# Reordering the decay blocks of a state-space scan on ScalarE and VectorE

## What is computed

```python
def ssd_scan(xs, dt, a, bm, cm, init_state):
    ...
    da_cs = jnp.cumsum(da, axis=-1)
    decay_in = jnp.exp(segsum(da))
    scores = jnp.einsum('bclhn,bcshn->bhcls', cc, bc) * decay_in
    y_diag = jnp.einsum('bhcls,bcshp->bclhp', scores, x)
    ...
    y = (y_diag + y_off).reshape(b, l, h, p)

def gated_rmsnorm(y, z, w):
    g = y.astype(jnp.float32) * jax.nn.silu(z.astype(jnp.float32))
    g = g.reshape(shape[:-1] + (SSD_GROUPS, SSD_WIDTH // SSD_GROUPS))
    g = g * lax.rsqrt(jnp.mean(g * g, axis=-1, keepdims=True) + EPS)
    return g.reshape(shape) * w.astype(jnp.float32)
```

## Time and profile before

| | |
|---|---|
| median of 3 runs | 763.07 us (762.62 to 763.31) |
| profiled execution | 761.61 us, span 759.9 us |
| TensorE busy | 723.8 us, 95% of the span |
| VectorE busy | 328.2 us, 43% |
| ScalarE busy | 215.9 us, 28% |
| GpSimd busy | 140.3 us, 18% |
| read from and written to HBM | 199.92 MB and 12.88 MB, 280 GB/s over the span |

### The profile page before, as it was taken

The page is one execution under the profiler, slowest core; times in us unless marked ns, Lnnn a source line. Parts: engine busy times, 40 slices in busy tenths (PEclk is TensorE's granted clock), DMA queues, the critical chain, the costliest instruction groups (busy, mean ns, idle before and its releaser), DMA issues.

```text
span 759.9 us, 10417 instructions
## 1 busy us (share of the span) xinstructions
PE 723.8 (95%) x3950; PEld 355.4 (47%) x3950; DVE 328.2 (43%) x880; ACT 215.9 (28%) x491; POOL 140.3 (18%) x234
## 2 busy tenths in 40 slices
PE   5999999999999999999999999999899899999995
PEld 4357553446445534433344755345544653443332
DVE  2022625647635552312471253474763555231157
ACT  2210155845024101011322024574602410111132
POOL 4146042220110100101102503322011011010112
PEclk9999999999999999999999999999999999999998
DMA  8999335997309799999896233497430379999962
GB/s 316 357 324 353 112 117 212 387 377 271 111 1 343 306 412 415 424 418 424 315 387 239 88 110 118 173 388 306 158 113 3 133 305 411 419 421 419 424 252 83
DMA packets 65655, 207.95 MB, mean 274 GB/s; under 512 B 8089, under 2 KB 8961, under 8 KB 53315
## 3 DMA queue, kind: packets, MB, share of 16 engines
q1 hardware_dynamic: 54936, 179.86, 61.2%
q10 hardware_dynamic: 5547, 16.12, 5.5%
q0 software_dynamic: 5120, 11.28, 4.4%
HBM read 199.92 MB, written 12.88 MB: 280 GB/s over the span
## 4 chain that ended last, share of the span: by engine, by line
PE 76%; DVE 9%; DMA 8%; ACT 3%; issue 2%; SPq 1%; POOL 1%; POOLq 0%; DVEq 0%; ACTq 0%
PE bank L2405 15%; PE bank L2290 11%; PE bank L2032 8%; PE bank L2420 7%; DMA arena<-in_w_up_dram 6%; PE bank L1976 6%; PE bank L2089 5%; PE bank L1897 4%; PE bank L2018 3%; DMA ring<-in_w_ada_dram 2%; PE bank L2134 2%; PE bank L2122 2%; PE bank L2396 2%; PE bank L2381 1%; PE bank L2106 1%
## 5 line engine op out<-in xcount | busy, mean ns | idle before, releaser
L2405 PE MATMUL bank<-ring,work 128*32 128x512 f32 (+1 forms) x640 | 114.2, 595 | 2.1 <-DMA arena<-in_w_up_dram 2.1
L2405 PEld LDWEIGHTS bank<-ring,work 128*32 128x32 f32 (+1 forms) x640 | 33.3, 120 | 73.8 <-issue 71.9
L1731 DVE COPY xs_tok<-bank 128x256 f32<-128x256 f32 x20 | 8.5, 425 | 135.5 <-PE bank L2412 135.5
L2420 PE MATMUL bank<-ring,xs_tok 128*64 128x512 f32 (+2 forms) x320 | 65.7, 597 | 1.0 <-DVE xs_tok L1731 1.0
L2032 PE MATMUL bank<-arena,ring 128*128 128x384 f32 x192 | 62.2, 486 | 0.0
L2405 PE MATMUL bank<-arena,work 128*64 128x512 f32 (+1 forms) x128 | 56.9, 597 | 0.0
L848 POOL DMA_INDIRECT gather_at<-h_rows,idx x18 | 18.2, 1013 | 173.1 <-PE bank L2396 130.7
L1897 PE MATMUL bank<-ring,cpad 128*32 128x512 f32 x384 | 49.7, 603 | 0.2 <-DMA ring<-in_w_ada_dram 0.2
L2032 PEld LDWEIGHTS bank<-arena,ring 128*128 128x128 f32 x192 | 36.5, 190 | 25.0
L1976 PE MATMUL bank<-ring,arena 128*128 128x512 f32 x96 | 42.8, 597 | 0.9 <-DVE arena L1278 0.5
L2290 PE MATMUL bank<-ring,arena 128*128 128x512 f32 x96 | 43.6, 597 | 0.0
(11 more groups left out here) (384 smaller groups left out, 1100.4 us busy)
## 6 DMA issues: line engine op xcount, KB each, us to landing
ring<-in_w_ada_dram SPq DMA_DIRECT2D x48, 1024.0 KB, 9.2
ring<-in_w_down_dram SPq DMA_DIRECT2D x28, 1024.0 KB, 14.1
ring<-in_w_gate_dram SPq DMA_DIRECT2D x24, 1024.0 KB, 12.1
ring<-in_w_up_dram SPq DMA_DIRECT2D x24, 1024.0 KB, 14.6
ring<-in_w_in_dram SPq DMA_DIRECT2D x15, 1024.0 KB, 13.9
ring<-in_w_out_dram SPq DMA_DIRECT2D x8, 1024.0 KB, 10.3
arena<-in_w_gate_dram SPq DMA_DIRECT2D x8, 1024.0 KB, 15.3
arena<-in_w_up_dram SPq DMA_DIRECT2D x8, 1024.0 KB, 17.9
```

What stands on the lines that cost most here:

```text
L2405: last = mm(bank[b][at:at + n, :].rearrange("p (i f) -> p i f", i=2), rows_T[:, kt * P + at:kt * P + at + n], gate_up_of(s)[:, kt, :, :], ...
L2420: last = mm(bank[5 + hf][at:at + n, :], hidT[:, b, f * P + at:f * P + at + n], w[:, f, hf * 512:(hf + 1) * 512], start=f == 0, stop=f == 1)
```

## The change

It has two parts. On ScalarE the exponential of block 1 goes ahead of the two copies, directly behind that of block 0; fall(2) stays right behind the copies. The two count functions follow the new order. On VectorE the scaling of a tile is split off from `finish` as `scaled`; for the first tile it goes from ahead of decayed(8) to behind decayed(9), for the other two it stays directly behind `finish`. No instruction is added or left out.

```diff
-        fall_at = lambda k: max(2 * k, 1)
-        exp_at = lambda k: min(2 * k + 3, 24)
+        fall_at = lambda k: 5 if k == 2 else max(2 * k, 1)
+        exp_at = lambda k: 4 if k == 1 else min(2 * k + 3, 24)
...
                 fall(0)
                 fall(1)
                 decay(0)
+                decay(1)
                 act.wait_ge(s_xtr, 5 * l + 4)
                 act.activation(b_tok.rearrange("p t c -> p (t c)"), bank[3][:, 0:NT * P], ACT.Copy).then_inc(s_xtc, 1)
                 act.wait_ge(s_xtr, 5 * l + 5)
                 act.activation(init_st[:, :, :].rearrange("p d c -> p (d c)"), bank[4][:, :],
                                ACT.Copy).then_inc(s_stc, 1)
-                for k in range(1, 12):
+                fall(2)
+                for k in range(2, 12):
                     if k < 11:
                         fall(k + 1)
                     decay(k)
...
                     ins.then_inc(s_gss, 1)
+
+                def scaled(t):
+
                     dve.wait_ge(s_grs, NT * l + t + 1)
                     for g in range(2):
-                        zg = z[:, g * 256:(g + 1) * 256]
+                        zg = mixed[:, t, 512 + g * 256:512 + (g + 1) * 256]
                         ins = dve.scalar_tensor_tensor(out=zg, in0=zg, scalar=grs[:, t, g:g + 1],
                                                        in1=snw[:, g * 256:(g + 1) * 256],
                                                        op0=ALU.mult, op1=ALU.mult)
...
                     if k == 7:
                         finish(0)
-                finish(1)
-                finish(2)
+                    if k == 9:
+                        scaled(0)
+                for t in (1, 2):
+                    finish(t)
+                    scaled(t)
```

## The result

| | before | changed |
|---|---|---|
| median | 763.10 us (6 runs, 761.66 to 763.31) | 757.85 us (6 runs, 757.31 to 758.98) |
| ratio | | 0.9937, 95% interval 0.9925 to 0.9950 |
| profiled execution | 761.61 us, span 759.9 | 757.44 us, span 755.7 |

The forecast was 759.5 (758.6 to 761.2): the right direction, and 1.6 us too little of a gain. The interval of the ratio stands for a gain of 3.8 to 5.7 us; the forecast was 3.6.

The account below looks back on a forecast made before the run. TensorE carries 76% of the span, so the gaps in the scans are what can be won: 0.50 + 1.11 + 0.50 + 1.61 - 0.12 = 3.6 us. Off the 763.07 us median that gave 759.5 us, range 758.6 to 761.2.

Parts of the forecast that it names:

- Rival 2: Expert stage: it ends on a weight stream that doesn't move and swallows the gain; 763.1 us, chance 0.08.
- Rival 3: Scans: the exponential's move works, but the power comes some 2 us late, decayed(10) stays; gain 1.0 us, 762.1, chance 0.04.
- rival 4: Scans: GpSimd's power, starved between VectorE's instructions, comes 3.7 us late; 2.4 us slower, 765.5, chance 0.04.
- Part 1: ScalarE, decay(1) ahead of the copies: TensorE's wait ahead of the first product goes, 0.50 us in each layer.
- Part 2: VectorE, first tile's scaling behind decayed(8) and decayed(9): decayed(10) comes 1.11 us earlier in layer 0, 1.61 in layer 1.
- The cost at the port: VectorE beside GpSimd: decayed(8) and decayed(9) lengthen, hidden in layer 0, 0 to 0.24 us in layer 1, taken as 0.12.
- rival 1: Exclusive port: GpSimd's pair starts only after decayed(8), costing 0.44 us in layer 0, 0.94 in layer 1; 760.8, chance 0.12.
- the sentence that the profile's gaps are what can be won: Scans: the projection behind them has no gap and starts as early as they let it, so only their gaps count.
- taking 3.6 off the median as off the profiled execution: Whole kernel: the same 3.6 us gain for both, 758.0 us for a profiled execution, 759.5 for the median.
- the only sign named: TensorE in the scan: a lower granted clock there would show the prediction wrong; no size given.

Follow-up runs that it names:

- part 1: Kernel before with only the exponential of block 1 moved ahead of ScalarE's two copies, VectorE as before: 761.79 us against 762.74, ratio 0.9989.
- the one with the PSUM input: Kernel before plus an unused VectorE product, one input in PSUM, in its wait for GpSimd's power: one execution, no time given; GpSimd's first instruction took 0.19 us.
- the one with two SBUF inputs: Kernel before plus an unused VectorE product, both inputs in SBUF, in its wait for GpSimd's power: one execution, no total time given; scaling some 0.45 us later.
- before, waits filled: Kernel before with idle TensorE products in the waits ahead of the fifth product of both layers: 761.91 us against 763.07, ratio 0.9987.
- part 1, waits filled: Kernel before with block 1's exponential ahead of the copies and idle TensorE products ahead of the fifth product: 760.58 us against 762.91, ratio 0.9968.
- part 2: Kernel before with only the first tile's scaling moved behind decayed(9), ScalarE as before: 759.77 us, ratio 0.9957.
- scaling further back: Changed kernel with modulation ahead of decayed(10), first tile's scaling behind decayed(11), its transposes behind the sixth product: 757.21 us, ratio 0.9930; again 757.96, 0.9933.

## Why the prediction was right or wrong

**Where the time is won: right.** Both parts worked at the places named, and nothing downstream took it back. Rival 2 (the weight stream swallows it) fell: the last expert unit's products came earlier by 1.95 us in layer 0 and 4.15 in layer 1, no less than the scans had given. Rival 3 and rival 4 (the power so late that it costs more than it brings) fell as well: the power ended at 183.45 in layer 0 and, in the profile shown in which it lost the race, at 542.30 in layer 1, where the scaling waited 0.59 us for it.

**Part 1: mechanism right, term 0.06 us too small in each layer.** I took the wait in the row, 0.50 us. Without a wait the next row starts some 0.06 us ahead of the end of the one before, so 0.56 us come back. The prediction had said "some hundredths more".

**Part 2: 1.11 and 1.61 us came out as 1.09 to 1.10 and up to 1.57**, with decayed(10) held by decay(10) and the scaling at once, as worked out.

**The cost at the port: the wrong victim and the wrong size.** I took the 0.92 us of decayed(0) as the price and let VectorE pay it, 0 to 0.24 us. At decayed(8) VectorE came first and GpSimd paid: 0.37 us in every profile of the changed kernel, always hidden. At decayed(9) in layer 1 GpSimd paid another 0.56 us in two of the three profiles of the changed kernel, and this the path does see. So rival 1 was right on the lock, and wrong to let GpSimd's pair hold up decayed(9) every time: in layer 0 decayed(9) comes 0.5 us after the power started, so the price there is nothing. In layer 1 the price is 0.04 or 0.6 us by a race, in place of my 0.12. That the scans of the first profile, 3.80 us, come so near to the 3.6 is in part luck: the race was won there.

**What was missing: the clock.** By the scans alone the gain is 3.8 us with the race won and 3.2 with it lost, in the mean of the three profiles 3.4, which is less than the 3.6 of the forecast. The measured one is larger: over all runs the kernel before has a mean of 762.97 (68 runs; the six of the first comparison, for which no clock is on record, are not among them), the changed one 758.38 (18 runs), 4.6 us with a standard error of 0.2.

The step that failed is the sentence that the profile's gaps are what can be won, together with taking 3.6 off the median as off the profiled execution. The sum has no term for a clock that falls behind a gap, no rival has one, and the only sign named was a lower clock after the change; it turned out higher (0.9963 against 0.9933 in the mean over the runs). The profiled execution of before was 1.5 us below the median, and I read that as spread. Its granted clock had held at 1.00 through both scans.

The other four profiles with the full wait ahead of the fifth product show half clock behind it in five of their eight scans: the second one of before and that of part 1 in layer 1, the one with the PSUM input in layer 0, the one with two SBUF inputs in both layers. The waits there were 0.91 to 1.77 us, and in the two profiles without an added VectorE product the fall cost 0.87 and 0.91 us. Of the ten scans with the full wait five held the clock, three with a wait of 0.83 us and two with 1.33 and 1.41 us, so the length alone doesn't decide. The nine profiles in which that wait is shortened or filled show no fall in a scan. The runs say the same:

| kernel | runs | mean us | mean granted clock |
|---|---|---|---|
| before | 68 | 762.97 | 0.9933 |
| before, waits filled | 12 | 762.07 | 0.9963 |
| part 1 | 12 | 761.82 | 0.9947 |
| part 1, waits filled | 12 | 760.67 | 0.9965 |
| part 2 | 7 | 760.02 | 0.9959 |
| changed | 18 | 758.38 | 0.9963 |
| scaling further back | 11 | 757.82 | 0.9959 |

Filling the waits gives 0.9 us (standard error 0.4) and 1.15 us (0.3) without touching the schedule. With 3.2 to 3.8 us of the scans that makes 4.1 to 5.0 us; measured 4.6. So the scans gave 0.2 us less than the forecast in the mean, and the clock about 1 us that the forecast did not have. Among the runs of the kernel before, the 16 with a mean clock above 0.9945 took 762.03 us and the 15 below 0.9925 took 764.55. Against the former the changed kernel is 3.65 us faster, near the forecast: the change was forecast for the execution that happened to be in the profile. This comparison picks runs by their clock and is no proof by itself. The 2.5 us between the two kinds of runs are more than two such falls cost, so late weights, behind which the clock fell as well in the profile above, may have a part in it. Nor does every row of the table fit closely: part 1 leaves the wait ahead of the fifth product as it was, and its mean clock is still 0.9947, while its gain, 1.15 us, is that of its scans alone.

What stays open: why the clock falls in one execution and not in another with the same wait, and the rest of the spread (about 0.7 us in the changed kernel), of which the 0.25 to 3.22 us of waiting for layer 0's last expert unit is a part. The 5.25 us of the first medians and the 4.6 of all runs both lie inside the first comparison's interval, 3.8 to 5.7, so the difference between them needs no cause of its own.

## What to carry to other kernels

When the profiled execution is faster than the median, ask what it was spared before taking its gaps for the whole price: here the second profile of the unchanged kernel showed it, and so did the granted clock of each run. A wait on TensorE like these (0.9 to 1.8 us in a stretch of small products) costs itself plus, in some executions, a stretch at half clock (0.9 us here), so removing it, or filling it with idle products, can pay more than its length. Only waits can be won: work moved to the other side of a wait on the same engine gave 0.06 us where I had expected 0.6. And before an instruction with two SBUF inputs is moved on VectorE, look at what GpSimd does at the new place, and whether the two come up together.

## What the runs showed of the hardware that I had not expected

- The granted clock fell from 1.00 to 0.50 (2.4 to 1.2 GHz) behind a wait of 1.33 us that followed a scan of small products, stayed there for about 3.4 us while TensorE was busy again, and did so in only some executions of one program. TensorE had stood at 0.66 us of busy time in the two us before. Over all profiles it fell behind five of ten such waits (0.83 to 1.77 us); behind the waits that the changed kernel has left ahead of the gate transposes (0.40 to 0.96 us) it did not in any of its three profiles. In a stretch of large products it fell behind a wait of 3.22 us for weights, and cost 1.70 us there.
- VectorE shuts GpSimd out while it reads two inputs from SBUF: GpSimd's instruction on two columns went from 0.19 to 0.56 us, its power from 0.70 to 1.25 us. With one of the inputs in PSUM they took 0.19 and 0.69 us. The other way round the power cost a VectorE product 0.04 us.
- A race of two instructions that come up within 0.01 us of each other moved the end of one scan by 0.56 us from one execution to the next (2.14 or 1.58 us gained).
